# Differential attention: scores of two token tiles in a row, another mean square, another order of the queues

## The chip, the cores and the metric

The kernel runs on one core of one Trainium2 chip. A core has TensorE (PE, matrix products into eight banks of PSUM; its weight loads are PEld), VectorE (DVE), ScalarE (ACT), GpSimd (POOL) and SyncE (SP, which only starts transfers here). Each engine works through its own queue in order, and the queues meet at semaphores. The metric is the time of one execution on the device in microseconds, the median of several runs; less is better.

## The reference, cut to what matters

The input x is 512 tokens of 1024 float32 values. Two layers follow one another. Layer 0 mixes tokens by a chunked gating network, layer 1 by differential attention; each is followed by a gated network with a width-3 convolution, and each of the four by a residual and a layer norm. The change lies in the attention of layer 1, which has 8 heads, each with two query and key pairs of 64 and a value of 128 columns:

```
q, k, v = split(x @ w_qkv)            # q, k: 8 heads x 2 x 64, v: 8 heads x 128
logits  = q[h, j] @ k[h, j].T         # j = 0, 1, for all 512 x 512 pairs
probs   = softmax(logits + bias[h])   # over keys
attn    = probs[j=0] - lam * probs[j=1]
o       = attn @ v[h]
o       = o * rsqrt(mean(o * o, over the 128 columns) + 1e-5) * subln_g * (1 - lambda_init)
out     = o @ w_out
```

## The kernel before, in words

Every large product is made from float32 data split into two F32R parts, `hi` (a rounded copy, made by ScalarE) and `lo` (the rest, a subtraction by VectorE or GpSimd). `product` (L1206) then issues three matrix products: hi with hi, and the two mixed ones. The plain float32 products are the transposes and the product with `ones` in `mean_square`.

In the attention the 512 tokens are four tiles of 128. Weights come in units of 1 MB through two buffers: SP loads a unit into `w_raw`, ScalarE makes `w_hi` (`weights`), GpSimd or VectorE makes `w_lo`, and TensorE waits for `w_lo_done` in `unit_ready`. For head h, in the loop over `H - 2` heads, all engines run an order written out by hand:

- TensorE (L1604 on): `turn_probs(h, k)` transposes the mixed probabilities of head h, four transposes for each k, into banks 5 and 6. `project(h + 2, c, ks)` makes the queries (c = 0, bank 0) and keys (c = 1, bank 1) of the head after next, three products of 512 columns for each of eight ks. `scores(h + 1, t)` makes the logits of query tile t for both j, in banks 2 and 3: the contraction is only 64 long, and j = 0 and j = 1 stand on different halves of the array's rows. `values(h, k)` sums attn @ v in bank 7. `mean_square(h)` multiplies `o_sq` by a matrix of 1/128, so that every row of bank 4 holds the mean.
- VectorE: `scored` adds the bias and takes the maximum while it reads the score banks; `weighed` takes the reciprocals of the sums; `mixed` makes the difference of the two probabilities; `probs_lo`, `query_key` and `values_lo` make low parts; `values` scales the output into `o_t`.
- ScalarE: `query_key` and `probs_hi` copy high parts, `exps` takes exponentials (two for a tile), `squares` squares bank 7 into `o_sq`, and `root` takes the inverse root by Ln and Exp, with a table load before each.
- GpSimd: `weights(u)` makes the low part of one weight unit in four pieces, `shares(h, t)` scales the probabilities of j = 0 by their sum's reciprocal; `mixed` waits for it.

In head 0 ScalarE's queue before has this order, and GpSimd makes `weights(U_QK1 + 1)`, the unit of head 2, after the four shares of head 0:

```
exps(0, 2)
values_hi(TB + 1)
exps(0, 3)
weights(U_QK1 + 1)
query_key(1, 0)
query_key(1, 1)
```

TensorE needs that unit at the first `project(2, 0, ...)`, behind two `turn_probs` of head 0. The last two heads stand behind the loop, with the values of heads 6 and 7 (`value_pair(U_V67, ...)`) and the first products of the output projection (`out_unit(U_BO, ...)`) in the place of the projections.

Of the kernel before, what the change touches and what calls it, by code (L numbers as in the profile page):

```python
# [45 lines left out]
def encoder_kernel(nc, x, positions, rel_bias_table, a_w_in, a_norm_g, a_norm_b, a_w_s, a_b_s,  # L46
# [85 lines left out]
    bias_sb = at("bias_sb", 112 * KB, [P, TB, S])  # L132
    qk_hi = at("qk_hi", R_S, [P, 2, 2, S], F32R)
# [33 lines left out]
    ones = tiny("ones", [P, P])  # L167
# [29 lines left out]
    with ExitStack() as ctx:  # L197
        bank = [ctx.enter_context(nc.psum_tensor(f"bank{b}", [P, NB], F32)) for b in range(8)]

        def sem(name):  # L200
# [38 lines left out]
        pv_mm, sq_done, ms_mm, ln_done, rs_o_done, o_done = (sem("pv_mm"), sem("sq_done"), sem("ms_mm"), sem("ln_done"),  # L239
                                                            sem("rs_o_done"), sem("o_done"))  # L240
# [5 lines left out]
        def qk_unit(h):  # L246
            return U_QK1 + h - 1 if h else U_QK0

# [167 lines left out]
        def _(act_e):  # L416
# [185 lines left out]
            def values_hi(n):  # L602
# [5 lines left out]
                else:  # L608
                    h, t = H // 2 + (n - TB) // 2 * 2, (n - TB) % 2 * 2
                    act_e.copy(val_hi[:, h:h + 2, t:t + 2, :].rearrange("p h t n -> p t h n"),  # L610
                               bank[(4 if n < TB + 2 else 0) + t // 2][:, :].rearrange("p (t h n) -> p t h n", t=2, n=P)
                               ).then_inc(bv_hi_done, 1)

            def query_key(h, c):

                act_e.wait_ge(q_mm if c == 0 else k_mm, h + 1)
                if h >= 2 and c == 0:
                    act_e.wait_ge(sc_mm, 2 * TB * (h - 1))
                act_e.activation(qk_hi[:, h % 2, c, :], bank[c][:, :], ACT.Copy,
                                 scale=HD ** -0.5 if c == 0 else 1.0).then_inc(qk_hi_done, 1)  # L620
# [8 lines left out]
            def probs_hi(h, k):  # L629
                act_e.wait_ge(at_mm, TB * h + k + 1)  # L630
                if k == 0 and h >= 1:
                    act_e.wait_ge(pv_mm, h)
                act_e.copy(at_hi[:, k, :], bank[5 + k % 2][:, :]).then_inc(at_hi_done, 1)

            def squares(h):
# [3 lines left out]
                act_e.activation(o_sq[:, :], bank[7][:, :], ACT.Square).then_inc(sq_done, 1)  # L639

            def root(h):
# [5 lines left out]
                act_e.activation(o_rs[:, :], bank[4][:, :], ACT.Ln, bias=eps_col[:, 0:1]).then_inc(ln_done, 1)  # L647
# [9 lines left out]
            weights(U_QK1)  # L657
            exps(0, 0)
            values_hi(TB)
            exps(0, 1)  # L660
            exps(0, 2)
            values_hi(TB + 1)
            exps(0, 3)
            weights(U_QK1 + 1)
            query_key(1, 0)
            query_key(1, 1)
            for h in range(H - 2):
# [7 lines left out]
                query_key(h + 2, 0)  # L675
                exps(h + 1, 2)
                squares(h)
                exps(h + 1, 3)
# [8 lines left out]
            exps(h + 1, 0)  # L687
            values_hi(TB + 2)
            exps(h + 1, 1)
            stationary(o_t, None, 0, o_done, 2)  # L690
            exps(h + 1, 2)
            values_hi(TB + 3)
            exps(h + 1, 3)
            weights(U_BO + 1)
            squares(h)
            stationary(o_t, None, 1, o_done, 4)
            h = H - 1
            probs_hi(h, 0)
            probs_hi(h, 1)
            root(h - 1)  # L700
# [20 lines left out]
        def _(dve):  # L721
# [319 lines left out]
            def values_lo(n):  # L1041
# [5 lines left out]
                else:  # L1047
                    h, t = H // 2 + (n - TB) // 2 * 2, (n - TB) % 2 * 2
                    dve.tensor_tensor(val_lo[:, h:h + 2, t:t + 2, :].rearrange("p h t n -> p t h n"),
                                      bank[(4 if n < TB + 2 else 0) + t // 2][:, :].rearrange("p (t h n) -> p t h n",  # L1050
                                                                                             t=2, n=P),
# [3 lines left out]
            def query_key(h, c):  # L1055
# [3 lines left out]
                if c == 0:  # L1059
                    ins = dve.scalar_tensor_tensor(out=lo, in0=bank[0][:, :], scalar=HD ** -0.5, in1=hi,  # L1060
                                                   op0=ALU.mult, op1=ALU.subtract)
                else:
                    ins = dve.tensor_tensor(lo, bank[1][:, :], hi, ALU.subtract)
                ins.then_inc(qk_lo_done, 1)

            def scored(h, t):
# [4 lines left out]
                for j in range(2):  # L1071
                    dve.wait_ge(sc_mm, 2 * TB * h + 2 * t + j + 1)
                    dve.tensor_tensor_reduce(prob[:, t, j, :], bank[2 + j][:, :], bias_sb[:, t, :], -1.0, 3.0e38,
# [29 lines left out]

            for n in range(TB):
                values_lo(n)
            query_key(0, 0)
            query_key(0, 1)
            scored(0, 0)
            weighed(0, 0)
            values_lo(TB)  # L1110
            scored(0, 1)
            mixed(0, 0)
            weighed(0, 1)
            scored(0, 2)
            mixed(0, 1)
            weighed(0, 2)
            values_lo(TB + 1)
            scored(0, 3)
# [3 lines left out]
            query_key(1, 0)  # L1122
            for h in range(H - 2):
                query_key(h + 1, 1)
                probs_lo(h, 0)
                probs_lo(h, 1)
                scored(h + 1, 0)
                probs_lo(h, 2)
                probs_lo(h, 3)
                weighed(h + 1, 0)  # L1130
                scored(h + 1, 1)
# [717 lines left out]
```

## Time and profile before

| what | value |
|---|---|
| median of 3 runs | 1295.48 us (1295.4 to 1296.23) |
| profiled execution | 1295.56 us |
| its span, first to last instruction | 1293.9 us |
| mean granted clock of TensorE | 0.998 |
| PE busy | 1277.3 us (99%) |
| PEld busy | 1051.6 us (81%) |
| DVE busy | 637.0 us (49%) |
| ACT busy | 456.7 us (35%) |
| POOL busy | 158.6 us (12%) |

All stretches below are counted in us from the start of the span of the profiled execution. A matrix product's duration in the timeline includes the time until its result has left the array, so successive products overlap, and the cost of one is read from start to start. A row with a count above 1 merges instructions that follow each other.

### The profile page before, as it was taken

What the parts mean: (1) busy time and instruction counts of PE and PEld (TensorE: products, weight loads), DVE (VectorE), ACT (ScalarE), POOL (GpSimd) and SP (SyncE); (2) the same over time, 40 slices, a digit from 0 to 9 for tenths busy, and PEclk for the clock granted to TensorE, in tenths of its full rate; (3) what the DMA queues carried; (4) which work ended last, traced back from release to release, by engine and by line L of the source; (5) the groups of instructions that cost most, each with busy time, mean ns of one, the idle gap of its engine ahead of it and who ended that gap; (6) DMA issues with size and microseconds to landing.
All of it is one profiled execution on the core that took longest, in us unless ns stands there. A gap on an engine that the chain in (4) does not pass through costs nothing.

```text
span 1293.9 us, 15596 instructions
## 1 busy us (share of the span) xinstructions
PE 1277.3 (99%) x6078; PEld 1051.6 (81%) x6078; DVE 637.0 (49%) x879; ACT 456.7 (35%) x545; POOL 158.6 (12%) x159
## 2 busy tenths in 40 slices
PE   8999999999999999999999999999999999999997
PEld 6788888889888888888888777788888888888886
DVE  3627877346343434433463566664743434343346
ACT  3422333322232323322314677776132323232230
POOL 3001100040000000000315442434200000000001
PEclk9999999999999999999999999999999999999999
DMA  8334563250322332222513334234132223323221
GB/s 300 105 98 115 176 174 139 93 184 1 130 97 97 97 97 97 98 97 94 166 58 92 105 88 114 82 115 152 44 98 97 97 97 96 99 93 102 94 101 65
DMA packets 103931, 140.62 MB, mean 109 GB/s; under 512 B 9360, under 2 KB 81128, under 8 KB 103632
## 3 DMA queue, kind: packets, MB, share of 16 engines
q1 hardware_dynamic: 94304, 127.67, 30.5%
q0 software_dynamic: 9440, 12.11, 2.9%
q8 instruction: 28, 0.46, 0.1%
q10 hardware_dynamic: 144, 0.26, 0.1%
q14 instruction: 15, 0.12, 0.0%
HBM read 137.85 MB, written 10.52 MB: 115 GB/s over the span
## 4 chain that ended last, share of the span: by engine, by line
PE 94%; DVE 4%; issue 1%; ACT 1%; DMA 0%; SPq 0%; DVEq 0%; ACTq 0%
PE bank L1208 31%; PE bank L1212 30%; PE bank L1211 30%; PE bank L1570 1%; PE bank L1224 1%; PE bank L1430 1%; DVE xt_lo L731 1%; PE bank L1594 1%; DVE x_tok L785 1%; DVE r_stat L754 0%; ACT xt_hi L436 0%; DMA w_raw<-in_a_w_in_dram 0%; DVE x_tok L748 0%; DVE x_tok L776 0%; PE bank L1433 0%
## 5 line engine op out<-in xcount | busy, mean ns | idle before, releaser
L1208 PE MATMUL bank<-xt_hi,w_hi 128*128 128x512 f32 (+1 forms) x1008 | 383.3, 380 | 0.4 <-DVE xt_lo L731 0.4
L1212 PE MATMUL bank<-xt_hi,w_lo 128*128 128x512 f32 (+1 forms) x1008 | 378.9, 376 | 0.0
L1211 PE MATMUL bank<-xt_lo,w_hi 128*128 128x512 f32 (+1 forms) x1008 | 378.8, 376 | 0.0
L726 DVE TENSOR_TENSOR w_lo<-w_raw,w_hi 128x2048 fp32r<-128x2048 f32 x79 | 180.8, 2288 | 190.5 <-ACT w_hi L431 164.1
L1208 PEld LDWEIGHTS bank<-xt_hi,w_hi 128*128 128x128 f32 x1008 | 189.7, 188 | 36.6 <-issue 3.0
L1211 PEld LDWEIGHTS bank<-xt_lo,w_hi 128*128 128x128 f32 x1008 | 189.8, 188 | 35.3 <-issue 1.4
L1212 PEld LDWEIGHTS bank<-xt_hi,w_lo 128*128 128x128 f32 x1008 | 189.7, 188 | 34.5
L431 ACT CAST w_hi<-w_raw 128x2048 fp32r<-128x2048 f32 x53 | 101.2, 1912 | 191.2 <-PE bank L1208 188.6
L1208 PE MATMUL bank<-w_hi,s_hi 128*128 128x512 f32 x416 | 162.5, 391 | 0.0
L1212 PE MATMUL bank<-w_hi,s_lo 128*128 128x512 f32 x416 | 161.9, 389 | 0.0
L1211 PE MATMUL bank<-w_lo,s_hi 128*128 128x512 f32 x416 | 161.9, 389 | 0.0
L1791 POOL TENSOR_TENSOR w_lo<-w_raw,w_hi 128x512 fp32r<-128x512 f32 x64 | 81.8, 1311 | 457.0 <-ACT w_hi L431 441.6
L585 ACT CAST w_hi<-w_raw 128x2048 fp32r<-128x2048 f32 x42 | 80.1, 1906 | 134.4 <-PE bank L1208 134.4
L1010 DVE SCALAR_TENSOR_TENSOR conv<-bank,conv_p,conv 128x511 f32<-128x511 f32 x44 | 33.0, 750 | 147.3 <-ACT conv L572 147.3
L572 ACT ACTIVATE conv<-bank,conv_p 128x512 f32<-128x512 f32 x44 | 34.3, 780 | 175.9 <-PE bank L1212 175.9
L1208 PEld LDWEIGHTS bank<-w_hi,s_hi 128*128 128x128 f32 x416 | 78.1, 188 | 16.6 <-issue 0.2
L1211 PEld LDWEIGHTS bank<-w_lo,s_hi 128*128 128x128 f32 x416 | 78.1, 188 | 16.3 <-issue 0.2
L1212 PEld LDWEIGHTS bank<-w_hi,s_lo 128*128 128x128 f32 x416 | 78.1, 188 | 16.2
L1208 PE MATMUL bank<-w_hi,xt_hi 128*128 128x512 f32 (+1 forms) x216 | 78.7, 364 | 0.6 <-DVE w_lo L832 0.6
L1027 DVE TENSOR_TENSOR act<-conv,bank 128x512 f32 (+1 forms) x44 | 30.2, 687 | 98.9 <-PE bank L1212 98.9
L1212 PE MATMUL bank<-w_hi,xt_lo 128*128 128x512 f32 (+1 forms) x216 | 77.3, 358 | 0.0
L1211 PE MATMUL bank<-w_lo,xt_hi 128*128 128x512 f32 (+1 forms) x216 | 77.3, 358 | 0.0
(191 smaller groups left out, 1411.9 us busy)
## 6 DMA issues: line engine op xcount, KB each, us to landing
w_raw<-in_f_w_in_dram SPq DMA_DIRECT2D x44, 1024.0 KB, 5.1
w_raw<-in_f_w_down_dram SPq DMA_DIRECT2D x22, 1024.0 KB, 4.8
w_raw<-in_a_w_in_dram SPq DMA_DIRECT2D x14, 1024.0 KB, 5.9
bias_by_query_key<-bias_by_distance POOLq DMA_DIRECT2D x8, 1024.0 KB, 15.5
w_raw<-in_a_w_out_dram SPq DMA_DIRECT2D x8, 1024.0 KB, 4.9
w_raw<-in_b_w_qkv_dram SPq DMA_DIRECT2D x16, 512.0 KB, 5.1
bias_sb<-bias_by_query_key SPq DMA_DIRECT2D x32, 256.0 KB, 2.6
w_raw<-in_b_w_qkv_dram SPq DMA_DIRECT2D x4, 1024.0 KB, 5.2
```

The source lines that it names most:

```text
L431: act_e.copy(hi_of(u), w_raw[:, u % 2, :]).then_inc(w_hi_done, 1)
L572: act_e.activation(conv[:, j, :], bank[j][:, :], ACT.Identity, bias=conv_col(l, NCP - 1, off + j), scale=conv_col(l, 1, off + j)).then_inc ...
L585: act_e.copy(w_hi[:, u % 2, :], w_raw[:, u % 2, :]).then_inc(w_hi_done, 1)
L726: dve.tensor_tensor(lo_of(u), w_raw[:, u % 2, :], hi_of(u), ALU.subtract).then_inc(w_lo_done, 1)
L731: ins = dve.tensor_tensor(xt_lo[:, 4 * h:4 * h + 4, t * P:t * P + P], bank[turn_bank(e, t) + h][:, :].rearrange("p (k n) -> p k n", n=P), ...
L785: return dve.scalar_tensor_tensor(out=x_tok[:, t, cols], in0=x_tok[:, t, cols], scalar=r_rs[:, t:t + 1], in1=ln_bc[:, 1, cols], op0=ALU.mu ...
L1010: dve.scalar_tensor_tensor(out=conv[:, j, 1:S], in0=bank[j][:, 0:S - 1], scalar=conv_p[:, l, bass.ds(off + j, 1)], in1=conv[:, j, 1:S], op ...
L1027: dve.tensor_tensor(dst, conv[:, j, :], bank[2 + j][:, :], ALU.mult).then_inc(act_done, 1)
L1208: ins = pe.matmul(o, a_hi, b_hi, start=start, stop=False)
L1211: pe.matmul(o, a_hi, b_lo, start=False, stop=False)
L1212: return pe.matmul(o, a_lo, b_hi, start=False, stop=stop)
L1791: ins = pool.tensor_tensor(lo_of(u)[:, part], w_raw[:, u % 2, part], hi_of(u)[:, part], ALU.subtract)
```

## The change

The diff does the following.

1. `scores` of two token tiles follow one another on TensorE, and use four banks: even tiles banks 2 and 3, odd tiles banks 1 and 4 (`score_bank`). They wait for the reads of two tiles back. The key projection moves from bank 1 to bank 2, the value pairs to banks 5, 6 and 0.
2. `mean_square` uses F32R: ScalarE squares bank 7 twice, into `o_sq` and rounded into `sq_hi`; VectorE makes `sq_lo` (`square_lo`); TensorE multiplies both by the F32R matrix `ones`, into bank 0 (bank 4 for the last two heads). `sq_hi` and `sq_lo` lie on the first part of `at_hi` and `at_lo`. More of the projection stands between `values` and `mean_square`: six blocks of three products instead of three such blocks.
3. `turn_probs(h, 2)` and `(h, 3)` follow one another, behind three such blocks instead of two.
4. The queues of VectorE and ScalarE follow that order. In head 0, `query_key(1, 0)` on ScalarE comes before `exps(0, 3)` and `weights(U_QK1 + 1)`.
5. GpSimd makes two pieces of a weight unit before the first share of a head, one after it, and one before the last share, from head 1 on.
6. Behind the loop, the order of value pairs, `values`, `out_unit` and `mean_square` is another.

```diff
+    sq_hi = at("sq_hi", R_U + 48 * KB, [P, S], F32R)
+    sq_lo = at("sq_lo", R_U + 56 * KB, [P, S], F32R)
-    ones = tiny("ones", [P, P])
+    ones = tiny("ones", [P, P], F32R)
+        def query_key_bank(c):
+            return bank[2 * c]
+        def score_bank(t, j):
+            return bank[(1, 4)[j] if t % 2 else 2 + j]
+        def pair_bank(n):
+            return bank[5 + n - TB if n < TB + 2 else 0]
+        def square_bank(h):
+            return bank[0 if h < H - 2 else 4]
...
             def squares(h):
                 act_e.wait_ge(pv_mm, h + 1)
                 if h >= 1:
                     act_e.wait_ge(ms_mm, h)
-                act_e.activation(o_sq[:, :], bank[7][:, :], ACT.Square).then_inc(sq_done, 1)
+                act_e.activation(o_sq[:, :], bank[7][:, :], ACT.Square)
+                if h >= H - 2:
+                    act_e.wait_ge(mixp_done, TB * (H - 1) + 1)
+                act_e.activation(squares_of(h)[0][:, :], bank[7][:, :], ACT.Square).then_inc(sq_hi_done, 1)
...
             weights(U_QK1)
+            values_hi(TB)
             exps(0, 0)
-            values_hi(TB)
             exps(0, 1)
+            values_hi(TB + 1)
             exps(0, 2)
-            values_hi(TB + 1)
+            query_key(1, 0)
             exps(0, 3)
             weights(U_QK1 + 1)
-            query_key(1, 0)
             query_key(1, 1)
...
+            def square_lo(h):
+                dve.wait_ge(sq_hi_done, h + 1)
+                hi, lo = squares_of(h)
+                dve.tensor_tensor(lo[:, :], o_sq[:, :], hi[:, :], ALU.subtract).then_inc(sq_lo_done, 1)
...
-                    if n >= 2:
-                        pe.wait_ge(sc_done, n - 1)
+                    if n >= 4:
+                        pe.wait_ge(sc_done, n - 3)
...
             def mean_square(h):
-                pe.wait_ge(sq_done, h + 1)
-                if h >= 1:
+                pe.wait_ge(sq_lo_done, h + 1)
+                if h < H - 2:
+                    pe.wait_ge(qk_lo_done, 2 * h + 5)
+                else:
+                    pe.wait_ge(sc_done, 2 * TB * H)
+                if h == H - 1:
                     pe.wait_ge(ln_done, h)
-                pe.matmul(bank[4][:, :], ones[:, :], o_sq[:, :], start=True, stop=True).then_inc(ms_mm, 1)
+                hi, lo = squares_of(h)
+                pe.matmul(square_bank(h)[:, :], ones[:, :], hi[:, :], start=True, stop=False)
+                pe.matmul(square_bank(h)[:, :], ones[:, :], lo[:, :], start=False, stop=True).then_inc(ms_mm, 1)
...
             for h in range(H - 2):
                 turn_probs(h, 0, 1)
                 turn_probs(h, 1)
-                project(h + 2, 0, range(0, 2))
+                project(h + 2, 0, range(0, 3))
                 turn_probs(h, 2)
+                turn_probs(h, 3)
                 scores(h + 1, 0)
-                turn_probs(h, 3)
-                project(h + 2, 0, range(2, 5))
                 scores(h + 1, 1)
+                project(h + 2, 0, range(3, 6))
                 values(h, 0)
-                project(h + 2, 0, range(5, KD))
+                values(h, 1)
                 scores(h + 1, 2)
-                values(h, 1)
+                scores(h + 1, 3)
                 values(h, 2)
-                scores(h + 1, 3)
                 values(h, 3)
-                project(h + 2, 1, range(0, 3))
+                project(h + 2, 0, range(6, KD))
+                project(h + 2, 1, range(0, 4))
                 mean_square(h)
-                project(h + 2, 1, range(3, KD))
+                project(h + 2, 1, range(4, KD))
...
             for h in range(1, H):
-                weights(U_QK1 + h + 1)
-                for t in range(TB):
-                    shares(h, t)
+                u = U_QK1 + h + 1
+                piece(u, 0)
+                piece(u, 1)
+                shares(h, 0)
+                piece(u, 2)
+                shares(h, 1)
+                shares(h, 2)
+                piece(u, 3)
+                shares(h, 3)
```

VectorE's queue in the loop after, where the prediction follows it, is `query_key(h + 1, 1)`, `probs_lo(h, 0)`, `(h, 1)`, `(h, 2)`, `scored(h + 1, 0)`, `probs_lo(h, 3)`, `scored(h + 1, 1)`, `weighed` 0 and 1, `scored(h + 1, 2)`, `mixed` 0, `scored(h + 1, 3)`, `mixed` 1, `weighed` 2, `square_lo(h)`, `query_key(h + 2, 0)`, `mixed` 2, `weighed` 3, `mixed` 3, `values(h)`. ScalarE's is `probs_hi` 0 and 1, the weights, `probs_hi` 2 and 3, `exps(h + 1, 0)` to `(h + 1, 2)`, `squares(h)`, `query_key(h + 2, 0)`, `exps(h + 1, 3)`, `root(h)`, `query_key(h + 2, 1)`. Behind the loop TensorE has after: turns 0 and 1 of head 6, value pair 0, turns 2 and 3, `scores(7, 0)` and `(7, 1)`, value pair 1, `scores(7, 2)` and `(7, 3)`, value pair 2, `values(6, 0)` and `(6, 1)`, value pair 3, `out_unit` of tile 1, `values(6, 2)` and `(6, 3)`, turns 0 and 1 of head 7, `out_unit` of tile 0, `mean_square(6)`, turns 2 and 3, and then as before.

## Rows read from the trace of the kernel before

**Rows 1.** The page: busy time by engine, and the clock row in 40 slices.
```profile
PE 1277.3 (99%) x6078; PEld 1051.6 (81%) x6078; DVE 637.0 (49%) x879; ACT 456.7 (35%) x545; POOL 158.6 (12%) x159
...
PEclk9999999999999999999999999999999999999999
```

**Rows 2.** Busy times (instructions) in one head: us, PE, PEld, DVE, ACT, POOL, clock, DMA.
```profile
744.61:765.54 20.93, 20.93 (x104) 15.18 (x103) 13.75 (x36) 15.57 (x28) 7.82 (x8) 1.00 0.36 101
```

**Rows 3.** Timeline of PE in that head: start us, us, engine, line, tiles, count.
```profile
744.45 1.03 PE L1570 MATMUL bank<-ident,prob 128*128 128x128 f32 x8
745.24 0.48 PE L1208 MATMUL bank<-xt_hi,w_hi 128*128 128x512 f32 x1
...
746.70 0.60 PE L1570 MATMUL bank<-ident,prob 128*128 128x128 f32 x4
747.23 0.50 PE L1208 MATMUL bank<-qk_hi 64*128 64x512 f32 x2
...
750.47 0.39 PE L1212 MATMUL bank<-xt_hi,w_lo 128*128 128x512 f32 x1
750.79 0.50 PE L1208 MATMUL bank<-qk_hi 64*128 64x512 f32 x2
...
751.68 0.50 PE L1208 MATMUL bank<-at_hi,val_hi 128*128 128x512 f32 x1
...
757.11 0.71 PE L1208 MATMUL bank<-qk_hi 64*128 64x512 f32 x2
...
761.07 1.02 PE L1594 MATMUL bank<-o_sq,ones 128*128 128x512 f32 x2
761.53 0.80 PE L1208 MATMUL bank<-xt_hi,w_hi 128*128 128x512 f32 x1
762.16 0.40 PE L1211 MATMUL bank<-xt_lo,w_hi 128*128 128x512 f32 x1
...
765.38 0.81 PE L1570 MATMUL bank<-ident,prob 128*128 128x128 f32 x6
```

**Rows 4.** Timelines of DVE and ACT in that head.
```profile
755.98 0.68 DVE L1073 CUSTOM_DVE_ANT_0 prob<-bank,bias_sb 128x512 f32<-128x512 f32 x1
...
757.19 0.75 DVE L1090 SCALAR_TENSOR_TENSOR prob<-prob,c 128x512 f32<-128x512 f32 x1
...
762.24 0.75 DVE L1090 SCALAR_TENSOR_TENSOR prob<-prob,c 128x512 f32<-128x512 f32 x1 [0.57 <-POOL prob L1797]
...
757.42 0.71 ACT L626 ACTIVATE prob<-prob,nmax 128x512 f32<-128x512 f32 x1
```

**Rows 5.** Timelines of PE, ACT and POOL in head 0.
```profile
712.47 0.50 PE L1208 MATMUL bank<-xt_hi,w_hi 128*128 128x512 f32 x1
...
724.29 0.47 PE L1208 MATMUL bank<-xt_hi,w_hi 128*128 128x512 f32 x1
...
715.06 1.90 ACT L431 CAST w_hi<-w_raw 128x2048 fp32r<-128x2048 f32 x1
718.25 0.60 ACT L619 ACTIVATE qk_hi<-bank 128x512 fp32r<-128x512 f32 x1 [1.30 <-PE bank L1212]
...
717.03 5.04 POOL L1791 TENSOR_TENSOR w_lo<-w_raw,w_hi 128x512 fp32r<-128x512 f32 x4 [0.89 <-ACT w_hi L431]
```

**Rows 6.** Timelines of DVE and POOL, and L740: ns min/median/max.
```profile
873.48 2.22 DVE L740 TENSOR_TENSOR s_lo<-o_t,s_hi 128x1024 fp32r<-128x1024 f32 x1 [2.25 <-ACT s_hi L451]
...
872.11 5.98 POOL L1791 TENSOR_TENSOR w_lo<-w_raw,w_hi 128x512 fp32r<-128x512 f32 x4 [1.67 <-ACT w_hi L431]
...
L740 DVE TENSOR_TENSOR s_lo<-o_t,s_hi x3: 1222/1225/2218, 864.2 to 897.1; 128x1024 fp32r<-128x1024 f32 x3
```

**Rows 7.** Timeline of PE in the last two heads.
```profile
872.56 1.12 PE L1594 MATMUL bank<-o_sq,ones 128*128 128x512 f32 x2
...
881.00 0.39 PE L1208 MATMUL bank<-at_hi,val_hi 128*128 128x512 f32 x1
```

**Rows 8.** Timeline of PE at the start.
```profile
9.50 1.91 PE L1353 MATMUL bank<-w_lo,xt_hi 128*128 128x512 f32 x4
```

More of the change, by code:

```diff
@@ L674, in _ @@
                 exps(h + 1, 1)
-                query_key(h + 2, 0)
                 exps(h + 1, 2)
                 squares(h)
+                query_key(h + 2, 0)
                 exps(h + 1, 3)
@@ L699, in _ @@
             probs_hi(h, 1)
+            stationary(o_t, None, 1, o_done, 4)
             root(h - 1)
@@ L1107, in _ @@
             query_key(0, 1)
+            values_lo(TB)
             scored(0, 0)
+            scored(0, 1)
             weighed(0, 0)
-            values_lo(TB)
-            scored(0, 1)
+            weighed(0, 1)
+            values_lo(TB + 1)
+            scored(0, 2)
             mixed(0, 0)
-            weighed(0, 1)
-            scored(0, 2)
+            scored(0, 3)
             mixed(0, 1)
             weighed(0, 2)
-            values_lo(TB + 1)
-            scored(0, 3)
+            query_key(1, 0)
             mixed(0, 2)
@@ L1126, in _ @@
                 probs_lo(h, 1)
+                probs_lo(h, 2)
                 scored(h + 1, 0)
-                probs_lo(h, 2)
                 probs_lo(h, 3)
+                scored(h + 1, 1)
                 weighed(h + 1, 0)
-                scored(h + 1, 1)
+                weighed(h + 1, 1)
+                scored(h + 1, 2)
                 mixed(h + 1, 0)
-                weighed(h + 1, 1)
-                query_key(h + 2, 0)
-                scored(h + 1, 2)
+                scored(h + 1, 3)
                 mixed(h + 1, 1)
                 weighed(h + 1, 2)
-                scored(h + 1, 3)
+                square_lo(h)
+                query_key(h + 2, 0)
                 mixed(h + 1, 2)
@@ L1146, in _ @@
             probs_lo(h, 1)
+            probs_lo(h, 2)
             scored(h + 1, 0)
-            probs_lo(h, 2)
             probs_lo(h, 3)
+            scored(h + 1, 1)
             weighed(h + 1, 0)
+            weighed(h + 1, 1)
             values_lo(TB + 2)
-            scored(h + 1, 1)
+            scored(h + 1, 2)
             mixed(h + 1, 0)
-            weighed(h + 1, 1)
-            scored(h + 1, 2)
+            scored(h + 1, 3)
             stationary(o_t, S_BO, 0)
@@ L1163, in _ @@
             mixed(h + 1, 3)
-            stationary(o_t, S_BO + 1, 1)
+            values_lo(TB + 3)
+            square_lo(h)
             h = H - 1
@@ L1167, in _ @@
             probs_lo(h, 1)
+            stationary(o_t, S_BO + 1, 1)
             values(h - 1)
@@ L1170, in _ @@
             probs_lo(h, 3)
+            square_lo(h)
             values(h)
@@ L1625, in _ @@
             turn_probs(h, 1)
-            value_pair(U_V67, 0, 0)
+            value_pair(U_V67, 0)
             turn_probs(h, 2)
+            turn_probs(h, 3)
             scores(h + 1, 0)
-            turn_probs(h, 3)
-            value_pair(U_V67, 0, 1)
             scores(h + 1, 1)
-            value_pair(U_V67, 0, 2)
+            value_pair(U_V67, 1)
             scores(h + 1, 2)
-            value_pair(U_V67, 0, 3)
             scores(h + 1, 3)
-            for k in range(TB):
-                values(h, k)
+            value_pair(U_V67, 2)
+            values(h, 0)
+            values(h, 1)
+            value_pair(U_V67, 3)
             out_ready(U_BO, S_BO, 0)
-            pe.wait_ge(bv_lo_done, TB + 4)
-            out_unit(U_BO, 0, (0,), start=True, frees=1)
-            mean_square(h)
+            pe.wait_ge(sc_done, 2 * TB * (H - 1) + 6)
+            out_unit(U_BO, 0, (1,), start=True, frees=1)
+            values(h, 2)
+            values(h, 3)
             h = H - 1
```

84 lines of the change are left out of this document (50 added, 34 removed).

## The prediction

> **What bounds the kernel now.** I read the page first: TensorE is busy for 1277.3 of 1293.9 us [rows 1], so only time taken from TensorE's own queue, or added to it as a wait, can move the end. Then the busy times by stretch: a head of the attention takes 20.93 us, TensorE is busy for all of it, VectorE for 13.75, ScalarE for 15.57 and GpSimd for 7.82 [rows 2]. Six heads run in the loop of L1604. Then the timeline of TensorE in one head, start against start, because the busy times overlap each other: there one sees what a switch from one kind of product to another costs. Last the timelines of the other engines, for how far their results come ahead of TensorE's need: the last `mixed` of a head ends at 762.24 + 0.75 = 762.99, the turns that need it start at 765.38 [rows 3, 4], 2.4 us of slack.
>
> **What the switches cost [rows 3].** In a run of projection products, 762.16 to 765.38 is 14 steps of 0.23 us. A score tile is six products, but its two halves stand on different 64 rows of the array and go in pairs, so 3 steps or 0.69. Around it: 0.32 from 750.47 to 750.79, 0.09 above a step; 0.89 inside (750.79 to 751.68) instead of 0.69, 0.20 above; the first product behind it lasts 0.50 where one within a run lasts 0.39, 0.11 above. That is 0.40 for a score block between full products. After four turns the scores start 0.53 later (746.70 to 747.23), where four turns are half of 0.79 (744.45 to 745.24, eight of them), so 0.13 at the entry, then 0.20 inside. The last block's first pair lasts 0.71 instead of 0.50: its second half waits some 0.22 for its bank to be read.
>
> **Part 1, two score tiles in a row, four banks.** Before, a head pays 0.33 + 0.40 + 0.40 + 0.62 = 1.75. After there are two blocks: 0.13 + 0.20 + 0.11 = 0.44 after turns, 0.40 between values, 0.84 in all. The price at the seam inside a block shows nowhere in this trace; below: 0, since inside a tile equal row halves follow at 0.23; above: a whole switch, 0.40. I take 0, the row inside a tile is the nearest. Gain 0.91. By the upper bound at both seams it would be 0.11. The Trainium skill (TensorEngine Tiling (Array Packing), Key Properties) says that TensorE drains when the tiling mode changes, not when only the tile does; the trace agrees with the first half, with 0.40 us at each change [rows 3], and by that rule the seam is free and the gain the full one. The four banks remove the 0.22: `scores` then waits for the tile two back.
> **Part 2, turns in pairs.** One switch from turns to a projection less: the product at 745.24 lasts 0.48 instead of 0.39. Gain 0.09.
> **Part 3, mean square.** The plain float32 product takes 0.46 to the next start (761.07 to 761.53), and the product behind it, with its two partners, 0.40 more than usual (it lasts 0.80 instead of 0.39): 0.86 in all. After, two F32R products of the size of a step, 0.46. Gain 0.40. F32R products of this shape are the trace's commonest, so the price is firm; bound above, no gain.
> Sum for a head: 0.91 + 0.09 + 0.40 = 1.40, so 20.93 becomes 19.5, and six heads give 8.4 us.
>
> **Whether the others keep up in 19.5.** Time 0 is the start of a head's turns. TensorE: turns 0 and 1 until 0.8, nine products until 2.9, turns 2 and 3 until 3.7, scores 0 and 1 from 3.8 to 5.4, projection until 7.6, values 0 and 1, scores 2 and 3 from 9.1 to 10.6, values 2 and 3 until 12.1, six products until 13.5, twelve until 16.3, mean square, twelve more, 19.5. I allow 0.2 until a result is seen. A tile's pair of reads on VectorE is 1.2 (755.98 to 757.19), a pair of exps 1.4 (two of 0.71), a copy 0.6 [rows 5], `mixed` 0.75 [rows 4]. Tile 0 is read from 4.9 to 6.1, tile 1 (after one `probs_lo`) from 6.8 to 8.0, exps of tile 1 end at 9.0, so scores 2 and 3 find their banks free at 9.1. Tile 2 is read from 10.1 to 11.3, `mixed` 0, tile 3 from 12.0 to 13.2, `mixed` 1, `weighed` 2 until 14.2. Now the new instructions. ScalarE squares twice from 12.3 (values are done) to 13.4, copies the query from 13.7 to 14.3, then the exps of tile 3 until 15.7. VectorE does `square_lo` until 14.8 and the query's low part until 15.5. Mean square wants both at 16.3: 0.8 to spare. Queued behind these two on VectorE: `mixed` 2 until 16.1, `weighed` 3, GpSimd's share until 17.0, `mixed` 3 until 17.8; the turns want it at 19.5: 1.7 to spare, from 2.4. The added 0.6 on ScalarE and 0.6 on VectorE are therefore covered, by the twelve projection products put ahead of the mean square; without that cover they would cost about 1 us a head. Root's last exp ends 0.2 after the turns start, 0.4 later than now, and the next low copies are needed at 2.9 and 3.4 and come at 2.3 and 2.9. GpSimd: two pieces (1.26 each, from 5.04 for four [rows 5]) from 3.5 to 6.0, the share of tile 0 at 8.2, piece 3 until 16.0, and the weights are due at 20.3 only. DMA queue: the bias rows and the next weights wait for the same reads of scores, which come 2 us earlier; piece 3's semaphore is not the one that holds the next load (that is one unit older).
> Contention: a VectorE subtraction of two SBUF tensors (L740, median 1.225 in the last two heads) took 2.22 at 873.48, while GpSimd subtracted, and four GpSimd pieces took 5.98 instead of 5.04 [rows 5, 6]. `square_lo` may meet the share of tile 2, `mixed` 2 meets piece 3. At 0.5 each, mean square has 0.3 to spare and the turns 0.7: still nothing.
>
> **Part 4, the order in head 0, where a new wait arises.** Before, ScalarE splits the weights of head 2 (`weights(U_QK1 + 1)`) at 715.06, before it copies query 1 at 718.25. After, its queue is `exps(0, 2)`, `query_key(1, 0)`, `exps(0, 3)`, `weights(U_QK1 + 1)`. The query copy waits for the whole projection of query 1: 718.25 - 712.47 = 5.78 after its start. Behind it: 0.49 for the copy to free the engine, two exps 1.44, so the split starts at +7.7, GpSimd 1.97 later (717.03 - 715.06) at +9.7, and its 5.04 end at +14.7. TensorE's `project(2, 0)` is due at 724.29 - 712.47 = +11.8 [rows 5]. It waits 2.9 us, once. Nothing else stands in its queue to fill the gap. Before, the low parts were there at 717.03 + 5.04 = 722.07, 2.2 ahead. GpSimd's new interleaving starts only at head 1 and does not help. In the first projections two seams are saved, 0.8.
>
> **Part 5, the last two heads.** Before, 0.33 + 3 x 0.40 = 1.53 for scores, after 0.84: 0.7. Turns 0.1. Two mean squares at 0.4: 0.8. New waits: the third value pair needs bank 0 read, and its copies stand behind the exps of tile 1, about 0.2 late; `values(7, 0)` needs `o_t` of head 6, whose mean square now comes only 4 us ahead of it instead of 8.4 (881.00 - 872.56 [rows 7]), while Ln, two table loads and exp take the time: about 0.3. Sum 1.1.
>
> **Sum.** 8.4 + 0.8 + 1.1 - 2.9 = 7.4. The profiled execution took 1295.56 (span 1293.9 and 1.7 around it), 0.1 above the median of 1295.48. Forecast 1295.56 - 7.4 = 1288.2, and since steps of 0.22 to 0.23 are read to 0.01, some 0.1 a head may be missing from the switches; I say 1287.8 us. Its own range is 1286 to 1289.5: the seam at up to 0.05 and the wait at 2.4 to 3.4.
>
> **Rivals.**
> A. The clock. After the 2.9 us of silence TensorE comes back at 1.2 GHz. The only rows that look like this are at the start of the trace: four products of 512 columns last 1.91 us there [rows 8], where four at 0.23 would last 3 x 0.23 + 0.39 = 1.08, so they are some 0.5 apart. If such a stretch is three times that long, 5.7 us bring half the work, so +2.9: 1290.7. For: there is no such idle time on TensorE behind the start, so the profile has not tried it. Against: the page's clock row stands at 9 tenths or more in all 40 slices [rows 1]. Chance 0.15. The Trainium skill (TensorE: Matmul & The Clock Gate, Part 1) says that the clock falls to half when TensorE has been idle; by that rule this rival comes true.
> B. The seam costs as much as a switch, 0.40, at 16 seams (12 in the loop, two each at its ends): +6.4, 1294.2, no measurable change. For: the halves' products go through one queue in order. Against: six products of a tile go at three steps. Half of it, 0.2, gives 1291.0. Chance 0.10 for half or more.
> C. `square_lo` comes too late, and TensorE waits before each mean square: with contention as in [rows 6] at its worst, 1.0 on it and 0.3 on the copies, 0.5 in each of six heads: +3, 1290.8. Against: 0.8 to spare. Chance 0.12.
> D. The other side: VectorE's chain becomes the bound. In a head it has five operations with two SBUF inputs between the first share and the next turns (`mixed` four times, `square_lo`). If each is stretched by 1.0 as L740 was, `mixed` 3 ends at 22.8 and a head takes 22.8: 6 x 1.9 = 11.4 slower, and with +2.9 of the wait, -0.8 and -1.1 it is 1308. It decides from a head of 20.8 us on (six heads then gain 0.8 to 1.0, which the 2.9 - 0.8 - 1.1 = 1.0 take back): (20.8 - 17.8) / 5 = 0.6 us on each of the five. Against: GpSimd works only 8 us in a head and meets two of them. Chance 0.04.
> E. The new wait does not arise, with everything else right: 1284.9. Nothing in the queues speaks for it. Chance 0.04.
> The forecast keeps 0.55. Range for 8 in 10: from 1285 to 1291, which takes in A, C and half of B. Within 0.2% (2.6 us, about what can be told from no change) is 1292.9 to 1298.1: 0.05, from B. Slower 0.05: D and what I have not seen. Faster 0.90.
>
> **What the profile after would show.** A wait of TensorE on GpSimd's `w_lo` (L1791) of 2.4 to 3.4 us near 724, once; 19.5 us a head; score blocks of 1.6 with no gap in them; two products of 0.23 for the mean square and none of 0.80 behind them; no wait for `square_lo`'s low part or `mixed` in the loop; a granted clock of 1.00 after the wait. I am wrong if the heads take over 20 us, if the wait is shorter than 2 us, or if it is followed by products at 0.43.

## The result, and the profile after

The changed kernel takes 1288.6 us (median of four executions, 1286.45 to 1288.93), the kernel before beside it 1295.44 (1295.3 to 1296.23). The ratio is 0.9945, with a 95% interval of 0.9933 to 0.9957: faster by 6.8 us, 0.55%. The forecast was 1287.8. The profiled execution took 1288.76, with a span of 1287.1 against 1293.9 [rows 1].

First the page after, with the line of busy times and the granted clock in 40 slices, and then windows: head 0, head 1 and head 5, each from the start of its turns to the start of the next head's. The columns are the length of the stretch, the busy times of PE, PEld, DVE, ACT and POOL with their counts, then the granted clock, the DMA share and GB/s.

```profile
PE 1267.7 (98%) x6078; PEld 1054.1 (82%) x6078; DVE 647.1 (50%) x887; ACT 459.2 (36%) x553; POOL 161.5 (13%) x159
...
PEclk9999999999999999999999999999999999999999
...
722.39:746.37 23.98, 21.34 (x103) 16.52 (x102) 14.45 (x35) 15.65 (x29) 11.93 (x11) 0.93 0.30 88
746.37:765.88 19.51, 19.51 (x104) 15.41 (x102) 15.11 (x36) 15.87 (x30) 8.32 (x8) 1.00 0.38 108
824.40:843.93 19.53, 19.53 (x104) 15.43 (x103) 15.11 (x36) 15.88 (x30) 8.32 (x8) 1.00 0.40 128
```

[Rows 2] gave 20.93 for a head. The other five now take 19.5 each (746.37 to 843.88 is 97.51 in all; the last window above ends 0.05 behind its head), with TensorE busy throughout. Head 0 takes 23.98, with 21.34 busy at a clock of 0.93. The page's clock row doesn't show this: a slice of it is 32 us long.

Next the timeline of TensorE in head 1 (start, duration, engine, line, operation), in the place of [rows 3]:

```profile
746.37 1.04 PE L1614 MATMUL bank<-ident,prob 128*128 128x128 f32 x8
747.17 0.47 PE L1246 MATMUL bank<-xt_hi,w_hi 128*128 128x512 f32 x1
...
749.33 1.04 PE L1614 MATMUL bank<-ident,prob 128*128 128x128 f32 x8
750.29 0.51 PE L1246 MATMUL bank<-qk_hi 64*128 64x512 f32 x2
...
750.87 0.40 PE L1250 MATMUL bank<-qk_hi,qk_lo 64*128 64x512 f32 x2
751.11 0.40 PE L1246 MATMUL bank<-qk_hi 64*128 64x512 f32 x2
...
751.90 0.50 PE L1246 MATMUL bank<-xt_hi,w_hi 128*128 128x512 f32 x1
...
755.53 0.50 PE L1246 MATMUL bank<-qk_hi 64*128 64x512 f32 x2
...
757.13 0.50 PE L1246 MATMUL bank<-at_hi,val_hi 128*128 128x512 f32 x1
...
762.70 0.39 PE L1643 MATMUL bank<-sq_hi,ones 128*128 128x512 f32 x1
762.93 0.39 PE L1644 MATMUL bank<-sq_lo,ones 128*128 128x512 f32 x1
763.15 0.39 PE L1246 MATMUL bank<-xt_hi,w_hi 128*128 128x512 f32 x1
```

Two tiles of scores go from 750.29 to 751.90 in 1.61. At the seam the second tile starts 0.24 after the last pair of the first (750.87 to 751.11), which is a step. The second block is 1.60. The 0.40 that the prediction counts is for a whole block, entry and exit, so about 0.20 for each switch between score products and full ones, and not 0.40 "at each change", as it says once. The mean square is two steps, 762.70 and 762.93, and the product behind it lasts 0.39, where it lasted 0.80.

What feeds those rows, on VectorE and then on GpSimd, in the same head, in the place of [rows 4]:

```profile
760.74 0.68 DVE L1137 TENSOR_TENSOR sq_lo<-o_sq,sq_hi 128x512 fp32r<-128x512 f32 x1
761.34 0.68 DVE L1089 SCALAR_TENSOR_TENSOR qk_lo<-bank,qk_hi 128x512 fp32r<-128x512 f32 x1
761.94 1.77 DVE L1119 SCALAR_TENSOR_TENSOR prob<-prob,c 128x512 f32<-128x512 f32 x1
...
764.61 0.75 DVE L1119 SCALAR_TENSOR_TENSOR prob<-prob,c 128x512 f32<-128x512 f32 x1 [0.58 <-POOL prob L1857]
...
760.67 1.24 POOL L1857 TENSOR_SCALAR prob<-prob,rsum 128x512 f32<-128x512 f32 x1 [3.31 <-DVE rsum L1109]
761.87 1.29 POOL L1845 TENSOR_TENSOR w_lo<-w_raw,w_hi 128x512 fp32r<-128x512 f32 x1
```

`square_lo` ends at 761.42 and the query's low part at 762.02, 0.7 ahead of the mean square. `mixed` 2 (761.94) starts beside a GpSimd piece (761.87) and takes 1.77 instead of 0.75. `mixed` 3 ends at 765.36, and the turns start at 765.88 (the fourth transpose is the first to need it): at least 0.5 to spare.

Last, head 0, by the timelines of ScalarE, GpSimd and TensorE, and by windows of TensorE's first products behind the gap, in the place of [rows 5]:

```profile
717.14 0.60 ACT L644 ACTIVATE qk_hi<-bank 128x512 fp32r<-128x512 f32 x1 [3.80 <-PE bank L1250]
...
719.04 1.90 ACT L456 CAST w_hi<-w_raw 128x2048 fp32r<-128x2048 f32 x1
...
721.02 7.64 POOL L1845 TENSOR_TENSOR w_lo<-w_raw,w_hi 128x512 fp32r<-128x512 f32 x6 [0.89 <-ACT w_hi L456]
...
722.39 1.04 PE L1614 MATMUL bank<-ident,prob 128*128 128x128 f32 x8
726.07 0.58 PE L1246 MATMUL bank<-xt_hi,w_hi 128*128 128x512 f32 x1 [2.65 <-POOL w_lo L1845]
726.45 0.63 PE L1249 MATMUL bank<-xt_lo,w_hi 128*128 128x512 f32 x1
...
729.82 1.04 PE L1614 MATMUL bank<-ident,prob 128*128 128x128 f32 x8
...
726.00:729.80 3.80, 3.73 (x9) 2.82 (x10) 0.00 (x0) 0.00 (x0) 2.52 (x3) 0.55 0.00 0
729.80:733.00 3.20, 3.20 (x24) 2.41 (x23) 1.77 (x4) 1.42 (x3) 0.00 (x0) 1.00 0.00 0
```

ScalarE copies query 1 at 717.14 and splits the weights of head 2 at 719.04. GpSimd makes their low parts from 721.02 on. TensorE's turns end at 722.39 + 0.79 = 723.18, its product starts at 726.07: 2.9 late, of which 2.65 is shown as idle. The nine products then take 3.75 to the next turns, where the nine in head 1 take 749.33 - 747.17 = 2.16, and they start 0.38 to 0.43 apart. The granted clock in that stretch is 0.55, so nearly all of it was at the lower level, 1.2 GHz; from 729.8 on it is 1.00.

The account, from the two profiled executions: everything up to head 0's turns 1.1 earlier (723.50 before, 722.39 after), of which 0.3 was there before the part that the change touches (a point at 685.71 before is at 685.39 after), so 0.8 is the change; head 0 longer by 3.0 (2.9 wait + 1.6 clock - 1.5 saved as in the others); five heads shorter by 7.35; from the end of head 5 on 1.4 (849.31 to 898.44 before, 843.88 to 891.63 after, both to the same point in the output projection). The sum is 6.8, the difference of the spans.

### The profile page after: what moved, and what is told of

Same layout as the page of the kernel before. It is cut to its first block, busy times and chain, and to the rows that moved or that the text cites. A ratio compares the mean times of both kernels' runs of the same rounds, so it can differ in the third digit from the quotient of the medians.

```text
span 1287.1 us, 15614 instructions
## 1 busy us (share of the span) xinstructions
PE 1267.7 (98%) x6078; PEld 1054.1 (82%) x6078; DVE 647.1 (50%) x887; ACT 459.2 (36%) x553; POOL 161.5 (13%) x159
## 4 chain that ended last, share of the span: by engine, by line
PE 93%; DVE 4%; ACT 1%; issue 1%; DMA 0%; POOL 0%; SPq 0%; DVEq 0%
PE bank L1246 30%; PE bank L1250 30%; PE bank L1249 30%; PE bank L1262 1%; PE bank L1614 1%; PE bank L1468 1%; DVE xt_lo L761 1%; DVE x_tok L815 1%; DVE r_stat L784 0%; ACT xt_hi L461 0%; DVE x_tok L778 0%; DMA w_raw<-in_a_w_in_dram 0%; POOL w_lo L1845 0%; DVE x_tok L806 0%; ACT prob L651 0%
```

## The experiments

The kernels start from the changed kernel; five of them take back the order of head 0 (on ScalarE and VectorE both), and one starts from the kernel before. Each ratio is against the kernel before, in the same session.

The executions of one kernel differ by 0.5 to 3 us. Much of what the profiled ones differ by arises ahead of the attention: the point at 685.71 in the profile before lies between 684.80 and 685.96 in the twelve profiles. From there to the turns of head 0 it is 37.79 us in both kernels with the old order of the scores and 36.98 to 37.00 in all ten others. So the rest of the span from that point on is given below as "the rest of the profile"; it compares single executions to about 0.1 us. It is 608.2 us before and 601.7 after.

**The change again**, for a second profile of the gap.

> The changed kernel once more, beside the others. Both theories: 1288.6 us as measured, with some executions near 1286.5 in which the products after the wait keep the full clock.

Measured: 1287.9 (1286.39 to 1289.16), ratio 0.9941 (0.9927 to 0.9954). TensorE in head 0:

```profile
725.56 0.80 PE L1246 MATMUL bank<-xt_hi,w_hi 128*128 128x512 f32 x1 [2.65 <-POOL w_lo L1845]
726.15 0.63 PE L1249 MATMUL bank<-xt_lo,w_hi 128*128 128x512 f32 x1
...
728.28 0.47 PE L1246 MATMUL bank<-xt_hi,w_hi 128*128 128x512 f32 x1
728.60 0.40 PE L1249 MATMUL bank<-xt_lo,w_hi 128*128 128x512 f32 x1
```

The wait is the same 2.65, but products are 0.43 apart only until 728.28. From 728.60 on they last 0.40, at full clock. The half clock lasted 2.7 us here, 3.75 in the first profile. The mean granted clock of each execution separates them: three with 0.997 took 1287.9 to 1289.2, two with 0.998 took 1286.4 and 1286.5. (Half a clock for 3.75 us is 0.0015 of a span of 1287.) In the first four executions of the changed kernel it is the same: 0.997 with 1288.4 to 1288.9, 0.998 with 1286.45. The rest of the profile is 601.3.

**ScalarE's order of head 0 taken back.**

```diff
-            query_key(1, 0)
             exps(0, 3)
             weights(U_QK1 + 1)
+            query_key(1, 0)
```

> Only ScalarE's order in head 0 goes back: exps(0, 3) and the weights before query_key(1, 0). Theory 1 (the unit's low part is late through the whole chain, VectorE and GpSimd too): GpSimd still stands behind share 3 of head 0, which waits for VectorE, whose queue still has query_key(1, 0) ahead of weighed(0, 3). GpSimd starts near 720.6 instead of 721.0, the gap on TensorE shrinks from 2.9 to about 2.5 us, and the time stays within 0.5 us of 1288.6. Rival (only ScalarE's split is late): GpSimd starts at 717.6, the gap is gone, 1283.9 us.

Measured: 1287.9 (1286.56 to 1289.32), ratio 0.9946 (0.9932 to 0.9959). VectorE, GpSimd and TensorE:

```profile
718.01 0.69 DVE L1089 SCALAR_TENSOR_TENSOR qk_lo<-bank,qk_hi 128x512 fp32r<-128x512 f32 x1 [2.51 <-ACT qk_hi L644]
...
719.53 0.69 POOL L1857 TENSOR_SCALAR prob<-prob,rsum 128x512 f32<-128x512 f32 x1 [3.48 <-DVE rsum L1109]
720.18 5.45 POOL L1845 TENSOR_TENSOR w_lo<-w_raw,w_hi 128x512 fp32r<-128x512 f32 x4
...
725.68 0.50 PE L1246 MATMUL bank<-xt_hi,w_hi 128*128 128x512 f32 x1 [2.02 <-POOL w_lo L1845]
726.02 0.40 PE L1249 MATMUL bank<-xt_lo,w_hi 128*128 128x512 f32 x1
```

Now the weights are split early, but GpSimd must first make a share at 719.53 whose `rsum` comes from VectorE, which stands at the query's low part (718.01) as before. The pieces start at 720.18 and TensorE is still 2.26 late. TensorE comes back with products a full step apart, and this execution has 0.998 and 1286.84; the other four have 0.997 and 1286.6 to 1289.3. The wait hangs on both queues, and taking back ScalarE's alone gives nothing measurable in the times (the wait is shorter by 0.6, less than their spread; the rest of the profile is 599.6, against 600.2 where the silence is filled). VectorE's alone was not run; in the changed kernel GpSimd waits last for ScalarE's split (0.89 at 721.02), so I would expect nothing of it either.

**Both orders taken back**: the same on VectorE, where `mixed(0, 2)`, `weighed(0, 3)` and `mixed(0, 3)` stand before `query_key(1, 0)` again.

```diff
-            query_key(1, 0)
             mixed(0, 2)
             weighed(0, 3)
             mixed(0, 3)
+            query_key(1, 0)
```

> ScalarE's and VectorE's order in head 0 go back, all else stays changed. Theory 1: GpSimd starts at 717.6 and ends at 722.7, 0.5 us before TensorE needs it at 723.2; the gap of 2.9 and the slow products behind it (9 at 0.43 instead of 0.23, 1.8) are gone: 1288.6 - 4.7 = 1283.9 us, and no execution is 2 us off the others. Rival (the half clock has nothing to do with the gap): 1288.6 - 2.9 = 1285.7 us.

Measured: 1284.0 (1283.13 to 1284.79), ratio 0.9911 (0.9896 to 0.9926). This is the best kernel of the study, 3.9 us below the change in the same session and 11.3 below the kernel before. GpSimd and TensorE:

```profile
717.99 5.48 POOL L1845 TENSOR_TENSOR w_lo<-w_raw,w_hi 128x512 fp32r<-128x512 f32 x4
...
722.96 1.04 PE L1614 MATMUL bank<-ident,prob 128*128 128x128 f32 x8
723.75 0.47 PE L1246 MATMUL bank<-xt_hi,w_hi 128*128 128x512 f32 x1
```

The pieces end at 717.99 + 5.48 = 723.47, and TensorE's product follows its turns at 723.75 with no wait: 0.3 to spare. Head 0 takes 19.50. No execution has a mean clock under 0.998. The 3.9 us lie between theory 1 (4.7) and the rival (2.9), and are what a clock that falls in some executions only would give. The rest of the profile is 597.1, 4.6 less than in the first profile of the change, where wait and clock were 2.9 + 1.6.

**The gap filled**: twelve products of 512 columns, whose sum the projection overwrites, in the place of the silence. (They add work that the output doesn't use, and so do the six of the last experiment.)

```diff
                 turn_probs(h, 1)
+                if h == 0:
+                    pe.wait_ge(qk_lo_done, 3)
+                    for n in range(12):
+                        pe.matmul(bank[0][:, :], xt_hi[:, n % KD, 0:P], xt_hi[:, n % KD, :], start=n == 0, stop=n == 11)
                 project(h + 2, 0, range(0, 3))
```

> The order stays changed, and twelve extra products of 512 columns (2.75 us), whose sum is overwritten, fill the gap of 2.9 us on TensorE. Theory 1 (the idle time brings the half clock): the next nine products stay at 0.23, 1.8 us less, 1286.8 us. Rival (the clock falls for another reason, or the gap is all there is): 1288.6 us, no change.

Measured: 1286.9 (1285.68 to 1287.07), ratio 0.9934 (0.992 to 0.9948).

```profile
722.72 3.01 PE L1661 MATMUL bank<-xt_hi 128*128 128x512 f32 x12
725.69 0.50 PE L1246 MATMUL bank<-xt_hi,w_hi 128*128 128x512 f32 x1
726.02 0.40 PE L1249 MATMUL bank<-xt_lo,w_hi 128*128 128x512 f32 x1
```

The product behind the filler comes at 725.69, as late as in the changed kernel, but is followed at a full step. With the wait kept and only the silence gone the median lies 1.0 below the change in the same session. The two intervals overlap, so the medians alone don't prove it; but the mean clock is 0.998 or 0.999 in all five executions, and none is above 1287.07. The rest of the profile is 600.2: 3.0 above the kernel with both orders taken back, which is the wait, and 1.5 below the first profile of the change, which is the clock. So the clock is a cost of its own beside the wait. GpSimd subtracts beside these products in both kernels (here from 720.57 to 728.31), so that isn't what slows them.

**The plain mean square**: both orders taken back, and one float32 product of `o_sq` by a float32 `ones`, as before. ScalarE's second square and `square_lo` stay.

```diff
-                pe.matmul(square_bank(h)[:, :], ones[:, :], hi[:, :], start=True, stop=False)
-                pe.matmul(square_bank(h)[:, :], ones[:, :], lo[:, :], start=False, stop=True).then_inc(ms_mm, 1)
+                pe.matmul(square_bank(h)[:, :], ones[:, :], o_sq[:, :], start=True, stop=True).then_inc(ms_mm, 1)
```

> Against the kernel with both orders back (1283.9 expected): the mean square is again one plain float32 product of o_sq, while ScalarE's second square and VectorE's square_lo stay in. Theory 1 (the F32R pair saves 0.40 on TensorE each time): 8 x 0.40 = 3.2 us more, 1287.1 us. Rival (the gain of the heads comes from the order alone): 1283.9 us.

Measured: 1287.6 (1287.19 to 1287.71), ratio 0.994 (0.9926 to 0.9954).

```profile
758.75 1.02 PE L1643 MATMUL bank<-o_sq,ones 128*128 128x512 f32 x2
759.20 0.80 PE L1246 MATMUL bank<-xt_hi,w_hi 128*128 128x512 f32 x1
```

It is 3.6 above the kernel with both orders taken back, measured in another session, and 3.2 above one that is equal to it up to GpSimd's order (below), in the same session: 0.40 to 0.45 for each of eight mean squares; the rest of the profile is 600.4, 3.3 more, 0.41 each. The rows show where (the one float32 product is entered as two): 0.45 to the next start, and the product behind lasts 0.80 again. Part 3 had 0.40.

**The scores apart**: both orders taken back, and three products between tiles 0 and 1, and a value tile between tiles 2 and 3.

```diff
                 scores(h + 1, 0)
+                project(h + 2, 0, range(3, 4))
                 scores(h + 1, 1)
-                project(h + 2, 0, range(3, 6))
+                project(h + 2, 0, range(4, 6))
...
                 scores(h + 1, 2)
-                scores(h + 1, 3)
                 values(h, 2)
+                scores(h + 1, 3)
```

> Against the kernel with both orders back (1283.9 expected): in the six heads of the loop one block of the projection stands between scores 0 and 1, and values 2 between scores 2 and 3. Theory 1 (each seam saves a whole switch, 0.40): 12 x 0.40 = 4.8 us more, 1288.7 us, no new wait. Rival (the gain came from the four banks, which stay): 12 x 0.0, 1283.9 us.

Measured: 1288.5 (1288.2 to 1289.35), ratio 0.9948 (0.9934 to 0.9961).

```profile
746.59 0.50 PE L1246 MATMUL bank<-qk_hi 64*128 64x512 f32 x2
...
747.49 0.50 PE L1246 MATMUL bank<-xt_hi,w_hi 128*128 128x512 f32 x1
```

A tile on its own takes 0.90 to the next product; two of them 1.80, against 1.60 in a row, and the product behind each is longer by 0.11. A head takes 20.36 instead of 19.50: 0.86 for two switches, 0.43 each (the rest of the profile, 602.4, is 5.2 more for twelve; the medians, 4.2 to 4.5 apart, give 0.35 to 0.38). Part 1 had 0.40. The rival is not all wrong: the fourth block (754.07 in that profile) takes 0.90 like the others, so the wait of 0.22 for its bank, which the kernel before had in each head, stays away with the four banks alone.

**The cover taken away**: both orders taken back, and three products instead of twelve of the key projection ahead of the mean square.

```diff
-                project(h + 2, 1, range(0, 4))
+                project(h + 2, 1, range(0, 1))
                 mean_square(h)
-                project(h + 2, 1, range(4, KD))
+                project(h + 2, 1, range(1, KD))
```

> Against the kernel with both orders back: in the loop only three instead of twelve products of the key projection stand ahead of the mean square. Theory 1 (the twelve products hide square_lo and the query's copies): TensorE reaches it 2.05 us earlier, 0.7 were to spare, so it waits 1.3 us a head, six times: 8 us more, 1292 us. Rival (the copies do not depend on this and come as early as they are asked for): no change.

Measured: 1293.5 (1292.39 to 1295.29), ratio 0.9989 (0.998 to 0.9998). The waits of TensorE (total, times, longest):

```profile
PE bank L1643 <- DVE qk_lo L1089: 8.0, 6, 1.4
```

Six waits of 1.3 us, one in each head of the loop, for the query's low part, which is queued on VectorE behind `square_lo`. Start to start each is 1.5 (as 2.65 was 2.9 in head 0), which is where the expectation fell short. A head takes 21.09, longer than before the change. The clock doesn't fall behind these waits: all eleven executions show 0.998 or 0.999. The new instructions of the mean square are free only because of the products ahead of it; without them all but 2 us of the kernel's gain is gone.

**GpSimd's order taken back**: both orders taken back, and a whole weight unit before the four shares.

```diff
-                piece(u, 0)
-                piece(u, 1)
-                shares(h, 0)
-                piece(u, 2)
-                shares(h, 1)
-                shares(h, 2)
-                piece(u, 3)
-                shares(h, 3)
+                weights(u)
+                for t in range(TB):
+                    shares(h, t)
```

> Against the kernel with both orders back: GpSimd makes all four pieces before the first share, as before the change. Theory 1 (the interleaving is off the path): pieces from 3.6 to 8.7 after a head's turns, share 0 half a us later, nothing waits: 1283.9 us, and mixed 2 no longer meets a piece, so it takes 0.75 instead of 1.77 us. Rival (the interleaving carries part of the gain): up to 0.5 us a head more, 1287 us.

Measured: 1284.4 (1283.3 to 1284.83), ratio 0.9914 (0.9901 to 0.9928), the same as with the new interleaving; so is the rest of the profile, 597.1. GpSimd and VectorE in one head:

```profile
756.38 1.23 POOL L1857 TENSOR_SCALAR prob<-prob,rsum 128x512 f32<-128x512 f32 x1 [4.17 <-DVE rsum L1109]
...
756.45 0.68 DVE L1137 TENSOR_TENSOR sq_lo<-o_sq,sq_hi 128x512 fp32r<-128x512 f32 x1
...
757.65 0.75 DVE L1119 SCALAR_TENSOR_TENSOR prob<-prob,c 128x512 f32<-128x512 f32 x1
```

`mixed` 2 takes 0.75 again, since no piece runs beside it; the share beside `square_lo` is still 1.23. In the loop the pieces' place changes VectorE's times and not the kernel's.

**The order alone**: the kernel before, with nothing of the change but the order of head 0 on ScalarE and VectorE.

```diff
             exps(0, 2)
             values_hi(TB + 1)
+            query_key(1, 0)
             exps(0, 3)
             weights(U_QK1 + 1)
-            query_key(1, 0)
```
(and `query_key(1, 0)` ahead of `mixed(0, 2)` on VectorE)

> The kernel before, with the change's order in head 0 alone (ScalarE: query_key(1, 0) ahead of exps(0, 3) and the weights; VectorE likewise). Theory 1: the wait of part 4 belongs to this order and to nothing else of the change: GpSimd ends at 727.2, TensorE needs it at 724.3, 2.9 us idle, and nine or fewer products at 0.43 behind it, up to 1.8: 1295.3 + 2.9 + 1.8 = 1300.0 us, between 1298.2 and 1300. Rival (the wait comes from the scores in a row, which end earlier and draw the projection forward): no change, 1295.3 us.

Measured: 1298.4 (1297.7 to 1300.07, eight executions), ratio 1.0028 (1.0017 to 1.0038).

```profile
722.64 1.04 PE L1570 MATMUL bank<-ident,prob 128*128 128x128 f32 x8
726.33 0.50 PE L1208 MATMUL bank<-xt_hi,w_hi 128*128 128x512 f32 x1 [2.65 <-POOL w_lo L1791]
```

The same wait of 2.65, 2.9 after the turns' end (722.64 + 0.79 = 723.43). The median is 3.0 above the kernel before, the wait alone; the rest of the profile, 611.2, is 3.0 more too. The profiled execution is the one of 1297.7; its product behind the wait lasts 0.50 as in a full-clock stretch, and the granted clock from 726.33 to 729.8 is 1.00. Four executions have a mean clock of 0.997 (1297.9, 1298.2, 1300.0, 1300.1) and four have 0.998 (1297.7 to 1298.6), so the clock falls here too, though by the times it cost something in two only. My expectation of 1300.0 put it into every execution.

**Half the gap filled**: the same edit with six products instead of twelve.

> The changed kernel with six extra products instead of twelve ahead of the late unit, so that TensorE is idle for 1.5 us instead of 2.9. Theory 1 (a long idle time brings the half clock, a short one does not): full clock behind it, 1286.8 us as with twelve. Rival (any idle time of this size brings it): up to 1.8 us more, 1288.6 us.

Measured: 1287.4 (1286.88 to 1287.79), ratio 0.994 (0.9927 to 0.9954).

```profile
723.34 1.63 PE L1661 MATMUL bank<-xt_hi 128*128 128x512 f32 x6
726.25 0.50 PE L1246 MATMUL bank<-xt_hi,w_hi 128*128 128x512 f32 x1 [1.29 <-POOL w_lo L1849]
```

TensorE is idle for 1.29 and comes back at full clock; the mean clock is 0.998 or 0.999 in all five executions. The median is 0.6 above what I expected and 0.5 above the kernel with the whole gap filled, which ran in another session, with overlapping intervals; the rest of the profile is 600.2 in both. So none of these five executions fell, where 14 of 22 did with the longer silence. That it is the length of the silence is likely (the six waits of 1.3 above brought no fall either) and not shown: the added products also change what TensorE did just before it.

## Why the prediction was nearly right

The time, 1288.6, lies within the likeliest case's own range and 0.8 above the forecast. But that is in part luck: a cost of 1.6 us left out was made up for by 1.0 that went the other way, and the median falls as it does because three of the four executions had the fall of the clock (the fourth took 1286.45).

- **Part 1 (0.91 a head)** held. The seam is a step (0.24), both blocks are 1.6, and the reverse experiment paid 0.43 for each added block on its own. Rival B is out.
- **Part 3 (0.40)** held: 0.40 to 0.45 for each mean square by the reverse experiment. Part 2 (0.09) was tested by nothing; the one product behind turns that is left lasts 0.47 (747.17), as in its sum. A head gained 1.47 instead of 1.40 by the account, so the 0.1 that I had left open as lost in rounding was mostly there.
- **The margins** held: 0.7 at the mean square, where I had 0.8 without contention and 0.3 with it, and 0.5 at the turns, where I had 1.7 and 0.7. Of the two new meetings with GpSimd `mixed` 2 paid 1.0 and `square_lo` nothing, where I had 0.5 on each. Rivals C and D are out. The cover was priced too low: "about 1 us a head" without the twelve products; with three of them left, it already cost 1.6 (21.09 - 19.50), nearly all of it the wait.
- **Part 4 (a wait of 2.9)** held in size, 2.9 in the profile and 2.9 to 3.0 by the order alone. Its cause was told by half: VectorE's queue makes GpSimd's share late in the same way (my working named only ScalarE's queue), and taking back ScalarE's order alone gave nothing measurable.
- **The step that failed** is in the sentences on what the profile would show: "a granted clock of 1.00 after the wait". By its own last words ("if it is followed by products at 0.43") the prediction was wrong there, and its sum has no term for it. Rival A came true, in smaller size and not always: 1.6 in the first profiled execution (3.75 - 2.16) and 1.3 in the second (729.06 - 725.56 = 3.5) instead of its 2.9, and nothing in some others. The argument against it, the 9s of the clock row [rows 1], could say nothing, because the kernel before has no such silence; the row shows 9s after the change too. The Trainium skill (TensorE: Matmul & The Clock Gate, Part 1) has the clock at half after TensorE has been idle, and makes that depend on how long it was, so the page doesn't by itself decide a silence of this size, as my sentence had it. Of the profiled executions with 2.65 us of idle time two agree with a fall (0.55 and 0.64 granted) and one, the order alone, doesn't (1.00).
- **Part 5 and the start**: 0.8 came as forecast (37.79 against 37.00); the last two heads gave 1.4 instead of 1.1, since `values(7, 0)` didn't wait for 0.3. Of the small waits there, the one for the value pair's copies is 0.2, as forecast; one of 0.25 for `s_lo` (871.79) was not foreseen.

So against the sum of 1288.2: +1.6 for the clock, -0.4 for the heads, -0.3 for the end, and -0.3 from the stretch ahead of the part that is changed, give 1288.8, the profiled execution.

## What to carry to other kernels

When instructions are put in another order on one queue, follow each result that it delays through every queue to the one engine that bounds the kernel: here one instruction moved ahead on each of two engines cost 3.9 us of the 11.3 that the rest of the change was worth; moving it back on ScalarE alone gave nothing measurable, on both everything. A silence on TensorE is to be counted at more than its length, because the products behind it may run at half clock; look at windows of a few us behind it, not at a row of 40 slices. A cost that is "hidden" should be tested by taking the cover away: here it was worth 1.6 us a head. And when two profiles are compared, find a point ahead of the change and count from there: here that left 0.1 of a spread of 0.5 to 3 us.

## What the runs showed of the hardware

- After 2.65 us of idle time TensorE came back at half clock in two profiled executions (0.55 granted over 3.8 us, 0.64 over 4.0 us) and at full clock in a third; after 2.02 and 1.29 us it was at full clock in the one profiled execution of each. Six waits of 1.3 us in one kernel brought no mean clock under 0.998 in eleven executions. A mean clock of 0.997 occurs in 14 of the 22 executions (four sets, of three kernels) with 2.0 to 2.7 us of silence, and in none of the 40 of the other experiments or the 36 of the kernel before beside them. The executions with 0.997 took 0.8 to 2.3 us longer on average than those with 0.998 of the same kernel. What decides in which execution the clock falls stays open.
- Where a VectorE operation with two SBUF inputs met a single GpSimd operation in the loop, one of the two was lengthened and not both: `mixed` 1.77 instead of 0.75, started 0.07 behind a piece of 1.29; a share 1.24 instead of 0.69 beside `square_lo`, which kept its 0.68. Where it met four pieces in a row, both were: `mixed` 1.77 and the pieces 5.48 instead of 5.04 (head 0 with both orders taken back), and likewise in [rows 6]. The Trainium skill (SBUF — State Buffer, SBUF: two separate sides) says of the ports that VectorE and GpSimd share that the one that starts first holds them to its end and the other waits. `mixed` agrees: its added 1.02 is most of the 1.22 that the piece still had. For the share the rows differ: it is written as started 0.07 ahead of `square_lo` and paid all the same, though starts on GpSimd are rough.
